# Stationary tiles of the expert stage at a pitch of 592 bytes in place of 512

## What is computed

```python
def swiglu(h, w1, w3, w2):
    return (jax.nn.silu(h @ w1) * (h @ w3)) @ w2

def moe_ffn(h, router, w1, w3, w2):
    logits = (h @ router).astype(jnp.float32)
    top_v, top_i = lax.top_k(logits, TOP_K)
    top_w = jax.nn.softmax(top_v, axis=-1)
    gates = jnp.sum(jax.nn.one_hot(top_i, N_EXPERTS, dtype=jnp.float32) * top_w[..., None], axis=-2)
    ...
    for e in range(1, N_EXPERTS):
        y = y + gates[..., e:e + 1] * swiglu(h, w1[e], w3[e], w2[e])
    return y
```

## Time and profile before

| | us |
|---|---|
| median of 3 runs | 1508.24 |
| lowest, highest | 1508.19, 1514.71 |
| span of the profiled execution | 1507.7 |
| TensorE busy (share) | 1480.4 (98%) |
| VectorE busy | 966.4 (64%) |
| ScalarE busy | 795.3 (53%) |
| moved by DMA | 488.76 MB, mean 324 GB/s |

### The profile page before, as it was taken

How to read it: one execution, slowest core, us unless ns; L and a number is a source line. 1 busy time by engine, 2 the same in 40 slices (tenths; PEclk the granted TensorE clock), 3 DMA queues, 4 the chain that set the end, 5 groups by cost and what they waited for, 6 DMA issues and landing times.

```text
span 1507.7 us, 19645 instructions
## 1 busy us (share of the span) xinstructions
PE 1480.4 (98%) x7706; PEld 1145.5 (76%) x7706; DVE 966.4 (64%) x897; ACT 795.3 (53%) x793; POOL 104.8 (7%) x101
## 2 busy tenths in 40 slices
PE   9999999999999999999999999999999999999996
PEld 8888889999898888878853588888834788888532
DVE  5856776454468667789930399898700798988301
ACT  4565636344354655487720387777501786877201
POOL 2000000000000000002200000200000000200041
PEclk9999999999999999999999999999999999999999
DMA  9655455788575544899999999999999999999996
GB/s 331 207 168 166 156 175 184 229 256 247 186 255 179 168 157 162 312 406 365 409 396 427 426 426 427 425 418 426 399 414 427 425 426 427 426 428 413 387 427 280
DMA packets 111788, 488.76 MB, mean 324 GB/s; under 512 B 8492, under 2 KB 12720, under 8 KB 68704
## 3 DMA queue, kind: packets, MB, share of 16 engines
q1 hardware_dynamic: 103520, 459.58, 78.5%
q0 software_dynamic: 7616, 27.47, 5.0%
q10 hardware_dynamic: 576, 0.61, 0.1%
HBM read 473.47 MB, written 15.21 MB: 324 GB/s over the span
## 4 chain that ended last, share of the span: by engine, by line
PE 86%; DMA 6%; DVE 3%; ACT 2%; SPq 2%; issue 1%; DVEq 0%; ACTq 0%
PE big L2022 14%; PE big L2017 14%; PE big L2018 14%; PE big L2561 7%; DMA eraw<-experts 6%; PE small L2022 6%; PE small L2017 5%; PE small L2018 5%; PE big L2096 4%; PE big L2103 4%; PE big L2097 4%; PE small L2124 3%; DVE elo L1407 2%; SPq L701 2%; PE small L2561 1%
## 5 line engine op out<-in xcount | busy, mean ns | idle before, releaser
L1407 DVE TENSOR_TENSOR elo<-eraw,ehi 128x2048 fp32r<-128x2048 f32 x210 | 475.7, 2288 | 69.6 <-ACT ehi L1121 55.0
L1121 ACT ACTIVATE ehi<-eraw 128x2048 fp32r<-128x2048 f32 x206 | 393.7, 1919 | 136.0 <-PE big L2022 63.6
L1311 DVE TENSOR_TENSOR wlo<-raw,whi 128x2048 fp32r<-128x2048 f32 (+2 forms) x104 | 229.9, 2217 | 143.5 <-ACT whi L903 142.6
L903 ACT ACTIVATE whi<-raw 128x2048 fp32r<-128x2048 f32 (+2 forms) x103 | 190.6, 1857 | 223.6 <-PE big L2022 82.9
L2017 PE MATMUL big<-ehi,hehi 128*128 128x512 f32 x560 | 219.9, 393 | 3.2 <-ACT ehi L1118 3.2
L2018 PE MATMUL big<-ehi,helo 128*128 128x512 f32 x560 | 218.1, 389 | 0.0
L2022 PE MATMUL big<-elo,hehi 128*128 128x512 f32 x560 | 150.4, 390 | 2.7 <-DVE elo L1407 2.7
L2017 PE MATMUL big<-whi,hhi 128*128 128x512 f32 (+1 forms) x384 | 151.9, 395 | 0.0
L2561 PE MATMUL big<-eraw,he 128*64 128x512 f32 (+1 forms) x768 | 147.6, 541 | 2.7 <-DMA eraw<-experts 2.7
L2018 PE MATMUL big<-whi,hlo 128*128 128x512 f32 (+1 forms) x384 | 149.0, 388 | 0.0
L1968 DVE TENSOR_TENSOR hid<-hid,big 128x512 f32<-128x512 f32 (+1 forms) x12 | 7.4, 621 | 207.2 <-PE big L2561 207.2
(11 more groups left out here) (407 smaller groups left out, 1868.2 us busy)
## 6 DMA issues: line engine op xcount, KB each, us to landing
eraw<-experts SPq DMA_DIRECT2D x336, 1024.0 KB, 16.9
raw<-ffn_w SPq DMA_DIRECT2D x30, 1024.0 KB, 5.9
raw<-w_gate SPq DMA_DIRECT2D x24, 1024.0 KB, 5.0
raw<-w_in SPq DMA_DIRECT2D x19, 1024.0 KB, 5.3
raw<-w_branch SPq DMA_DIRECT2D x12, 1024.0 KB, 5.0
raw<-w_o SPq DMA_DIRECT2D x8, 1024.0 KB, 5.0
xs_all<-zeros POOLq DMA_DIRECT2D x11, 512.0 KB, 7.0
raw<-w_in SPq DMA_DIRECT2D x4, 896.0 KB, 9.6
```

The source lines that it names most:

```text
L903: act.activation(whi[u % HI][:, 0:kt, 0:cols], raw[u % RAW][:, 0:kt, 0:cols], ACT.Copy).then_inc(hi_ready, 1)
L1121: act.activation(ehi[HI_OF[n]][:, :], eraw[n % RING][:, :], ACT.Copy).then_inc(ehi_ready, 1)
L1311: dve.tensor_tensor(wlo[u % RAW][:, 0:kt, 0:cols], raw[u % RAW][:, 0:kt, 0:cols], whi[u % HI][:, 0:kt, 0:cols].bitcast(F32), ALU.subtract) ...
L1407: dve.tensor_tensor(elo[n % RING][:, :], eraw[n % RING][:, :], ehi[HI_OF[n]][:, :].bitcast(F32), ALU.subtract).then_inc(elo_ready, 1)
```

## The change

Seven tiles are placed anew. `hehi`, `helo`, `eahi` and `ealo` get 148 columns a block in place of 128, of which the last 20 are never written or read: their pitch is 592 bytes, so that the blocks start 80 bytes further from a multiple of 512 each time. All instructions that write or read these tiles take columns 0 to 127 of each block; those at lines 1143 and 1897 therefore write four rows of 128 columns where they wrote one of 512. To make room, `Gg` and `GT` move behind `eahi` into the place of the attention's tables, and `lgT` into that of `hlo`. `last_hi` and `last_lo` stay as they were. What lies behind the moved tiles shifts: `he32` now starts 128 bytes past a multiple of 512.

```diff
--- before.py
+++ after.py
@@ -47,6 +47,8 @@
 
 
 SLOT = P
+
+PITCH = SLOT + 20
 EXTRA = 2 * TOKENS // (SLOT + 1)
 SLOTS = NE + EXTRA
 MORE = -(-TOKENS // SLOT) - 1
@@ -374,23 +376,24 @@
         eraw = [w(f"eraw{i}", a, [P, 2048]) for i, a in enumerate(at_unit)]
         elo = [w(f"elo{i}", a, [P, 2048], F32R) for i, a in enumerate(at_unit)]
         o += 8192 * (E_GATES + E_MERGED)
-        hehi = w("hehi", o, [P, KD, SLOT], F32R)
-        helo = w("helo", o + 4096, [P, KD, SLOT], F32R)
-        Gm = w("Gm", o + 8192, [P, NB, SLOT])
-        Gg = w("Gg", o + 9216, [P, NB, SLOT])
-        GT = w("GT", o + 10240, [SLOT, NB, P])
-        o += 11264
+        hehi = w("hehi", o, [P, KD, PITCH], F32R)
+        helo = w("helo", o + 4 * KD * PITCH, [P, KD, PITCH], F32R)
+        Gm = w("Gm", o + 8 * KD * PITCH, [P, NB, SLOT])
+        o += -(-(8 * KD * PITCH + 1024) // 512) * 512
 
         ysb = at("ysb", over_h + 8192, [SLOT, D])
         hid = at("hid", over_h + 12288, [SLOT, PAIR])
-        eahi = at("eahi", over_mask, [P, 8, SLOT], F32R)
+        eahi = at("eahi", over_mask, [P, 8, PITCH], F32R)
+        Gg = at("Gg", over_mask + 4 * 8 * PITCH, [P, NB, SLOT])
+        GT = at("GT", over_mask + 4 * 8 * PITCH + 1024, [SLOT, NB, P])
+        assert 4 * 8 * PITCH + 2048 <= 4 * (HEADS + 1) * SCORE
         xs = xn[:, 0, :]
         ea32 = at("ea32", over_mask, [P, 8, CAP])
         last32 = at("last32", over_xn + 4096, [P, 4, CAP])
         last_hi = at("last_hi", over_xn + 4096, [P, 4, SLOT], F32R)
         last_lo = at("last_lo", over_xn + 6144, [P, 4, SLOT], F32R)
         place[0] = work + o
-        lgT = keep("lgT", [P, TOKENS])
+        lgT = at("lgT", over_h + 8192, [P, TOKENS])
         lg = keep("lg", [P, NB, NE])
         pair = keep("pair", [P, NB, NE * NE])
         pair2 = keep("pair2", [P, NB, NE * NE])
@@ -421,7 +424,7 @@
         ones = keep("ones", [P, P])
         gfin = keep("gfin", [P, D])
         place[0] = -(-place[0] // 512) * 512
-        ealo = keep("ealo", [P, 8, SLOT], F32R)
+        ealo = keep("ealo", [P, 8, PITCH], F32R)
         he32 = keep("he32", [P, KD, CAP])
         mark = keep("mark", [P, 1])
         counts = keep("counts", [P, NE])
@@ -631,7 +634,7 @@
 
             if p == PAIRS - 1:
                 return last_hi[:, :, :], last_lo[:, :, :]
-            return eahi[:, :, :], ealo[:, :, :]
+            return eahi[:, :, 0:SLOT], ealo[:, :, 0:SLOT]
 
         def light_tiles(p):
 
@@ -1125,7 +1128,7 @@
                 act.wait_ge(gather_done, 2 * (s - 1) + i + 1)
                 for k in range(4):
                     c = G_ROUTE + 4 * i + k
-                    a = act.activation(hehi[:, 4 * i + k, :], gather_place(i, k), ACT.Copy, scale=pcol[:, c:c + 1])
+                    a = act.activation(hehi[:, 4 * i + k, 0:SLOT], gather_place(i, k), ACT.Copy, scale=pcol[:, c:c + 1])
                 a.then_inc(hehi_ready, 1)
 
             def outputs(s):
@@ -1140,7 +1143,8 @@
 
                 act.wait_ge(hid_turned, HE * wides_before(s) + t + 1)
                 hi, _ = turn_tiles(t)
-                act.activation(hi.rearrange("p a n -> p (a n)"), small[:, turn_bank(t), :], ACT.Copy).then_inc(ahi_ready, 1)
+                src = small[:, turn_bank(t), :].rearrange("p (a n) -> p a n", n=SLOT)
+                act.activation(hi, src, ACT.Copy).then_inc(ahi_ready, 1)
 
             def slot(s, first=False):
                 for n in range(UNITS):
@@ -1250,7 +1254,7 @@
 
             for k in range(KD):
                 act.wait_ge(first_gather, k // 2 + 1)
-                a = act.activation(hehi[:, k, :], first_place(k), ACT.Copy, scale=pcol[:, G_ROUTE + k:G_ROUTE + k + 1])
+                a = act.activation(hehi[:, k, 0:SLOT], first_place(k), ACT.Copy, scale=pcol[:, G_ROUTE + k:G_ROUTE + k + 1])
                 if k % 2:
                     a.then_inc(first_hehi, 1)
             slot(0, first=True)
@@ -1784,8 +1788,8 @@
                 dve.wait_ge(hehi_ready, 2 * (wides_before(s) - 1) + i + 1)
                 for k in range(4):
                     c = G_ROUTE + 4 * i + k
-                    d = dve.scalar_tensor_tensor(helo[:, 4 * i + k, :], gather_place(i, k), pcol[:, c:c + 1],
-                                                 hehi[:, 4 * i + k, :].bitcast(F32), ALU.mult, ALU.subtract)
+                    d = dve.scalar_tensor_tensor(helo[:, 4 * i + k, 0:SLOT], gather_place(i, k), pcol[:, c:c + 1],
+                                                 hehi[:, 4 * i + k, 0:SLOT].bitcast(F32), ALU.mult, ALU.subtract)
                 d.then_inc(he_ready, 1)
 
             def gate_values():
@@ -1885,8 +1889,8 @@
             unit_lo(0, 1)
             for k in range(KD):
                 dve.wait_ge(first_hehi, k // 2 + 1)
-                d = dve.scalar_tensor_tensor(helo[:, k, :], first_place(k), pcol[:, G_ROUTE + k:G_ROUTE + k + 1],
-                                             hehi[:, k, :].bitcast(F32), ALU.mult, ALU.subtract)
+                d = dve.scalar_tensor_tensor(helo[:, k, 0:SLOT], first_place(k), pcol[:, G_ROUTE + k:G_ROUTE + k + 1],
+                                             hehi[:, k, 0:SLOT].bitcast(F32), ALU.mult, ALU.subtract)
                 if k % 2:
                     d.then_inc(first_he, 1)
 
@@ -1894,8 +1898,8 @@
 
                 dve.wait_ge(ahi_ready, HE * wides_before(s) + t + 1)
                 hi, lo = turn_tiles(t)
-                dve.tensor_tensor(lo.rearrange("p a n -> p (a n)"), small[:, turn_bank(t), :],
-                                  hi.rearrange("p a n -> p (a n)").bitcast(F32), ALU.subtract).then_inc(alo_ready, 1)
+                src = small[:, turn_bank(t), :].rearrange("p (a n) -> p a n", n=SLOT)
+                dve.tensor_tensor(lo, src, hi.bitcast(F32), ALU.subtract).then_inc(alo_ready, 1)
 
             def slot(s, first=False):
                 for n in range(UNITS):
@@ -2469,7 +2473,7 @@
                     hi, lo = unit_view(ehi[HI_OF[n]], n), unit_view(elo[n % RING], n)
                     halves = range(pair_width(p) // 512 if m < 2 else 2)
                     out = big[m] if m < 2 else small
-                    xhi, xlo = (hehi, helo) if m < 2 else hidden_tiles(p)
+                    xhi, xlo = (hehi[:, :, 0:SLOT], helo[:, :, 0:SLOT]) if m < 2 else hidden_tiles(p)
                     first_t, last_t = (0, KD - 1) if m < 2 else (0 if p == 0 else -1, tiles * q + tiles - 1 if n == UNITS - 1 else -1)
 
                     def high(half, k):
```

## The result

The changed kernel takes 1519.8 us (median of 7 runs, 1518.2 to 1521.6) against 1509.0 for the kernel before, run beside it: ratio 1.0067, 95% interval [1.0053, 1.0081]. It is slower by 0.67%, about 10 us. The forecast was 1497 with a range from 1492 to 1512; the time lies outside and on the other side, at the 1520 of rival C.

The account below looks back on a forecast made before the run. TensorE was taken to pace the wide slots and transfers the light ones; gains of 3 + 3.7 + 4.7 = 11.4 us from 1508.2 gave 1496.8, rounded 1497 us, range 1492 to 1512.

Parts of the forecast that it names:

- rival C: Expert stage: walking starts keep products at the unsettled 231.7 ns; 12.0 us lost, 1520 us, chance 0.16.
- the two bounds: Expert-stage products on the four re-pitched tiles: between 26.6 us won and 12.0 us lost over five wide slots.
- the lower bound's side: The side taken: products fall to the fp32 rows' 215.6 ns, 5.3 us a wide slot if TensorE were the only limit.
- the unsettled start: First products of slot 0: 231.7 ns each, 18.4 ns lost, before the pace settles at 226.7 ns.
- The fp32 rows: Plain fp32 products, cqnT on wuq: 215.6 ns a record, 2.3 ns lost, read as a load hidden almost without loss.
- light slots: Three of the expert stage's eight slots, ending paced by DMA; he32 there was priced at 0.
- The upper bound: Wide slots: products never settle and cost 231.7 ns each, 5.0 x 480 x 5 = 12.0 us lost.
- wide pair: Two neighbouring wide slots of the expert stage, 2 and 3 or 5 and 6, paced by TensorE; each predicted 10.6 us saved before caps.
- slot 0: First wide slot of the expert stage: only its second half is TensorE's own, so about 3 us gained.
- Rival B: The start does not matter or the gain is too small: 1508 us, 1504 to 1512, chance 0.37.
- The caps: Gain limited to the time transfers stood still: 3.7 us in slots 2 and 3, 4.7 in slots 5 and 6.
- The other edits at 0: Gapped writes of eahi and ealo, moved Gg, GT and lgT, and he32's new start were each priced at 0.

Follow-up runs that it names:

- off80: Changed kernel with pitch 512 bytes and hehi, helo, eahi and ealo each starting 80 bytes in: 1519.7 us, ratio 1.0062.
- he768: Changed kernel with hehi and helo at a pitch of 768 bytes, Gm moved behind GT, one rounding 256 for 512: 1509.3 us, ratio 0.9999.
- p512: Changed kernel with the same placement and instructions but a pitch of 512 bytes: 1509.6 us, ratio 1.0004.
- off256: Changed kernel with pitch 512 bytes and hehi, helo, eahi and ealo each starting 256 bytes in: 1509.5 us, ratio 0.9994.
- lo80: Changed kernel with pitch 512 bytes and only helo and ealo starting 80 bytes in: 1515.8 us, ratio 1.0040.
- all96: Kernel before the change with every tile of the arena 96 bytes further: 1513.8 us, ratio 1.0029.
- all96_st256: Changed kernel with all tiles 96 bytes further and the expert stage's four stationary tiles another 160: 1524.4 us, ratio 1.0096.

## Why the prediction was wrong

**The step that failed** is the choice between the two bounds in "The change part by part": "I take the lower bound's side, because the loss behaves like a collision of streams with the same alignment". The two streams do depend on each other through their addresses, but with the sign turned round: the common alignment was the good case, and each start off it costs more: 232.5 ns a product where this step had 215.6. The rows could not carry the choice. They showed a dependence on timing at a single alignment; I read it as the harm of that alignment, when it could as well be the sign of a settled, favourable state., the unsettled start, had the size of the changed kernel's price: 231.7 ns there, 232.5 ns after. Their tiles are aligned, so their loss has another cause than the distance, and it is in part luck that the two agree. The fp32 rows said nothing of fp32r products: the light slots' plain fp32 products take 19.03 us for 88 records both with he32 aligned and with he32 128 bytes off (772.47 above), so these at least do not react to the distance.

**Bounds.** The upper bound held: 12.0 us by 5.0 x 480 x 5, measured 11.1 us of span. The 4.7 us of a wide pair over its 960 products are 4.9 ns each; units differ, from 2.77 us (901.84 to 904.61) to the 2.79 shown, which is 5.8 ns a product. In slot 0 1.1 us came of 2.4, since there the split of the weights shared the pace, and this was the argument that I used for a gain and not for a loss; the first light slot's 0.5 us stood in no bound.

**Rival C** had the time (1520) and the place, and the wrong reason. It said that a walk keeps the products from settling. Offsets without a walk cost the same (off80), and a walk by 256 bytes costs nothing (he768). What is shown: a load whose start is a multiple of 256 bytes from the start of the moving block leaves 226.7 ns; every other distance that was tried, constant (80, 128, 160 bytes) or walking in steps of 16, 64 or 80, gives 231 to 233 ns. Why the distance counts, for instance by banks that both streams meet, is argued and not shown: no run looks into the memory.

**Rival B** rested on the earlier trace rows: doubling the pitch to 1024 changed nothing. The row was right and too narrow. 512 and 1024 are both multiples of 256, and the test that it seemed to be was none.

**The Trainium skill's sentence** that TensorE's two read ports are independent and that it never waits on anyone (SBUF — State Buffer, Who interferes with whom) does not agree with these runs as far as it is taken for a sum of 0: by the address of the load alone a product went from 226.7 to 232 ns. The measurement decides.

**The caps.** The 3.7 and 4.7 us were limits to a gain and were not tested. That nothing caps a loss held: the light slots' DMA stretches did not shrink.

**The other edits at 0** held: 1.0004 for the whole placement (p512). he32's start costs nothing either: its 88 records take 19.03 us at the old start and 128 bytes off it, and off256 (0.9994) has it 256 bytes off.

**The range** ended at 1512 and left most of C out at a chance of 0.16. With a capped gain of 11.4 us on one side, a loss of 12.0 on the other and no row to choose by, it should have reached 1520.

No version beats the kernel before: p512, off256 and he768 tie with it.

## What to carry to other kernels

Place the stationary tiles of fp32r products so that each block starts a multiple of 256 bytes from the moving block it is used with; 512 columns then take 226.7 ns and otherwise 232, 2.5%; at 448 and 256 columns no loss was seen, nor on plain fp32 products. Padding against an imagined conflict made it worse here. And a pattern seen at one alignment says that something depends on timing, not which way another alignment will go: put both signs into the range, or find a row at a second alignment that is really different.

## What the runs showed of the hardware that was not expected

- The pace of an fp32r product of 512 columns depends on the distance between the start of its neighbour's load and its own moving data, modulo 256 bytes: 226.7 ns at 0, 231 to 233 ns at the others tried, in the expert stage and outside it; products of 256 columns keep 120.0 ns on average at either distance, and eight of 448 columns 1.63 us. Plain fp32 products from a tile 128 bytes off keep 19.03 us for 88 records.
- One off load in two is enough to slow all products of the run (lo80: 232.5 ns for eight in a row), and aligned loads bring the pace back within a few products.
- Tiles that start 96 bytes past a multiple of 512 lower the ceiling of the transfers into them: 421 and 422 GB/s against 426 and 427, in rows of 8192 bytes a partition at full DMA share, in all96 and all96_st256 alike. It made the kernel 0.29% slower [0.19%, 0.38%] with the products unchanged.
